# A hybrid convolution, attention and expert block on one core: channel tile 0 of the convolution moved to two other engines, and four edits to the start and the passes of the expert stage

## The reference

```python
u = rms_norm(x, norm1_g)
proj = u @ w_in                        # 1024 conv columns, 512 q, 128 k, 128 v
val, gate = proj[..., :512], proj[..., 512:1024]
z = val * sigmoid(gate)                # GLU
z = causal_depthwise_conv(z, conv_w) + conv_b      # 31 taps, 512 channels
conv_out = silu(layer_norm(z))
attn_out = swa_sink_attention(q, k, v) # 8 heads, chunks of 64, window of two chunks
h = x + concat(conv_out, attn_out) @ w_out
v = rms_norm(h, norm2_g)
gates, experts = softmax(top4(v @ router_w + router_b))        # 32 experts
y = h + sum over the 4 experts of gate * (clamped_swiglu(v @ w1[e] + b1[e]) @ w2[e] + b2[e])
```

## Time and profile before

| | |
|---|---|
| median of three runs | 2154.91 us |
| the profiled execution | 2154.91 us, its span from the first to the last instruction 2153.2 us |
| busy: PE, DVE, ACT, POOL | 2020.3, 932.0, 397.5, 228.1 us |
| chain that ended last | PE 82%, DVE 10%, issue 3%, ACT 2%, DMA 1%, POOL 1% |
| chain by line | PE L1001 46%, PE L1041 11%, PE L1016 10%, DVE L740 5% |
| start of the passes | 561.59 us after the span's start |

### The profile page before, as it was taken

One profiled execution on the slowest core, in us unless ns is written; L12 is line 12 of the kernel. 1 busy time (PEld: TensorE's weight loads), 2 busy tenths in 40 slices (PEclk: granted clock), 3 DMA queues, 4 the chain that ended last, 5 costly groups with the idle time before them and its releaser, 6 DMA issues.

```text
span 2153.2 us, 34646 instructions
## 1 busy us (share of the span) xinstructions
PE 2020.3 (94%) x13213; PEld 1648.4 (77%) x13214; DVE 932.0 (43%) x2247; ACT 397.5 (18%) x849; POOL 228.1 (11%) x223
## 2 busy tenths in 40 slices
PE   5997887899799999999999999999999999998997
PEld 3444543444677887788878887999999999988997
DVE  2895667333444444444443444333333333333221
ACT  3113334311111111111111111121111111110111
POOL 3101110000101010011101010011000000000000
PEclk9998889998799999999999999999999999999999
DMA  5020003212599899998999899988788887775651
GB/s 224 1 78 0 1 1 134 87 66 99 195 328 336 304 327 329 337 326 305 327 338 332 298 338 328 322 286 300 275 279 275 279 280 260 267 266 166 237 176 41
DMA packets 226274, 492.44 MB, mean 229 GB/s; under 512 B 7469, under 2 KB 8009, under 8 KB 226224
## 3 DMA queue, kind: packets, MB, share of 16 engines
q1 hardware_dynamic: 207504, 431.24, 55.5%
q0 software_dynamic: 16768, 59.98, 10.2%
q10 hardware_dynamic: 1952, 0.49, 0.1%
HBM read 458.88 MB, written 32.80 MB: 228 GB/s over the span
## 4 chain that ended last, share of the span: by engine, by line
PE 82%; DVE 10%; issue 3%; ACT 2%; DMA 1%; POOL 1%; ACTq 0%; DVEq 0%; POOLq 0%
PE bank L1001 46%; PE bank L1041 11%; PE bank L1016 10%; DVE arena L740 5%; PE bank L1215 5%; PE bank L1335 2%; PE bank L1136 1%; PE bank L1120 1%; ACT arena L543 1%; PE bank L1269 1%; PE bank L1029 1%; DVE arena L769 1%; DVE arena L785 1%; DVE mx L774 1%; PE bank L1307 1%
## 5 line engine op out<-in xcount | busy, mean ns | idle before, releaser
L1001 PE MATMUL bank<-arena 128*128 128x128 f32 (+5 forms) x8192 | 998.4, 284 | 21.5 <-issue 21.5
L1001 PEld LDWEIGHTS bank<-arena 128*128 128x128 f32 x8192 | 989.3, 192 | 34.1 <-issue 34.1
L663 DVE TENSOR_SCALAR arena<-bank,b1c 128x256 f32<-128x256 f32 x256 | 123.8, 483 | 611.1 <-PE bank L1001 602.0
L430 ACT ACTIVATE arena<-arena 128x256 f32<-128x256 f32 x256 | 106.6, 417 | 866.7 <-DVE arena L663 784.0
L1041 PE MATMUL bank<-arena 128*128 128x512 f32 x576 | 262.1, 593 | 0.0
L1016 PE MATMUL bank<-arena 128*128 128x144 f32 (+4 forms) x1792 | 252.0, 294 | 4.6 <-DVE arena L675 4.4
L1016 PEld LDWEIGHTS bank<-arena 128*128 128x128 f32 x1792 | 237.1, 190 | 7.8 <-DVE arena L675 7.7
L973 DVE TENSOR_SCALAR arena<-bank,cols 128x256 f32<-128x256 f32 x256 | 112.1, 480 | 283.4 <-PE bank L1335 283.4
L320 POOL DMA_INDIRECT out<-arena,idx_cur x64 | 99.0, 1547 | 826.9 <-ACT arena L444 422.5
L1041 PEld LDWEIGHTS bank<-arena 128*128 128x128 f32 x576 | 102.5, 190 | 94.7 <-issue 90.4
L740 DVE SCALAR_TENSOR_TENSOR arena<-arena,cols 128x1024 f32<-128x1024 f32 x120 | 159.3, 1328 | 3.7 <-ACT arena L518 0.2
(11 more groups left out here) (222 smaller groups left out, 1108.8 us busy)
## 6 DMA issues: line engine op xcount, KB each, us to landing
arena<-in_w SPq DMA_DIRECT2D x192, 2048.0 KB, 11.9
arena<-in_x SPq DMA_DIRECT2D x16, 512.0 KB, 5.2
token_rows<-arena SPq DMA_DIRECT2D x8, 528.0 KB, 5.9
arena<-in_w_in SPq DMA_DIRECT2D x2, 2048.0 KB, 11.2
out<-arena SPq DMA_DIRECT2D x8, 512.0 KB, 2.9
arena<-in_w_in SPq DMA_DIRECT2D x1, 3072.0 KB, 23.3
arena<-in_w_out SPq DMA_DIRECT2D x1, 2048.0 KB, 9.5
arena<-in_w_out SPq DMA_DIRECT2D x2, 1024.0 KB, 15.6
```

The source lines that it names most:

```text
L430: a.activation(sg[:, m % 2, :], g1[:, m % 2, :], ACT.Sigmoid, scale=ALPHA).then_inc(sg_ready, 1)
L663: v.tensor_scalar(g1[:, r, :], bank[r][:, 0:SLOTS], b1c[:, m:m + 1], LIMIT, ALU.add, ALU.min).then_inc(g1_ready, 1)
L1001: last = mm(bank[m % 2][:, side * SLOTS:side * SLOTS + n], w1_sb[:, k, lo:lo + P], xT[:, k, 0:n], start=k == 0, stop=k == KD - 1)
```

## The change

1. Channel tile 0 of the convolution leaves DVE. ACT writes tap 0 as before and then, for each other tap, a copy of zT scaled by the weight into one of two new buffers, `tapped`; POOL adds it to cT[:, 0] (1024 tokens). The 30 adds stand in groups of five behind units 2 to 7 of `glu`, on both engines. DVE keeps tiles 1 to 3, now with their tap 0 too, a tensor_scalar. 49 of its 93 taps stand before the attention. Behind `norm_qk(0)` DVE waits for the last add.
2. SP no longer waits for the first gather before it loads the w2 of the first pass.
3. `add_b2` of the last tile stands ahead of the index list's end on DVE instead of behind it.
4. The xT of the first pass is taken out by DVE behind the table instead of by ACT beside it. PE does transposes 1 to 3 behind the table's second matmul.
5. `down_rows` of half b waits for `yt_ev` at q2 + b instead of q2.

```diff
+        tapped = [part(9.5, SEQ), part(23.5, SEQ)]
+        FIRST_TAPS = [(1 + 5 * max(i - 2, 0), 1 + 5 * max(i - 1, 0)) for i in range(2 * CT)]
@@ SP
             sp.wait_ge(wo_mm, 2 * NT)
-            sp.wait_ge(gath_in, 32)
             for c in range(2):
                 load_w2(sp, c, 0)
@@ POOL
             for i in range(2 * CT):
                 glu(i)
+                for j in range(*FIRST_TAPS[i]):
+                    pool.wait_ge(tap_ready, j + 1)
+                    if j >= 2:
+                        pool.wait_ge(tap_added, j - 1)
+                    pool.tensor_tensor(cT[:, 0, :], cT[:, 0, :], tapped[j % 2], ALU.add).then_inc(tap_added, 1)
@@ ACT, in unit i
-                if i % 2 == 1:
-                    c = i // 2
-                    a.wait_ge(z_ready, i + 1)
-                    a.activation(cT[:, c, :], zT[:, c, 0:SEQ], ACT.Identity, scale=col(CW + c * WIDTH), bias=col(CB + c)
-                                 ).then_inc(first_tap, 1)
+                for j in range(*FIRST_TAPS[i]):
+                    z = zT[:, 0, j:j + SEQ]
+                    if j == 1:
+                        a.wait_ge(z_ready, 2)
+                        a.activation(cT[:, 0, :], zT[:, 0, 0:SEQ], ACT.Identity, scale=col(CW), bias=col(CB)
+                                     ).then_inc(tap_ready, 1)
+                    if j >= 3:
+                        a.wait_ge(tap_added, j - 2)
+                    a.activation(tapped[j % 2], z, ACT.Copy, scale=col(CW + j)).then_inc(tap_ready, 1)
@@ ACT, ahead of the passes
-            for i in range(2):
-                a.wait_ge(h_out[i], 16 * (NT // 4))
-            for i in range(4):
-                a.wait_ge(xt_mm, i + 1)
-                (two activations into xT, then_inc(xt_ev, 1))
@@ DVE
-            taps = [(c, j) for c in range(CT) for j in range(1, WIDTH)]
+            taps = [(c, j) for c in range(1, CT) for j in range(WIDTH)]
             def tap(c, j):
-                if j == 1:
-                    v.wait_ge(first_tap, c + 1)
+                if j == 0:
+                    v.wait_ge(z_ready, 2 * (c + 1))
+                    link(v.tensor_scalar(cT[:, c, :], zT[:, c, 0:SEQ], col(CW + c * WIDTH), col(CB + c), ...))
...
-            some_taps(2 * (WIDTH - 1) + 9)
+            some_taps(WIDTH + 18)
             norm_qk(0)
+            v.wait_ge(tap_added, WIDTH - 1)
...
             one_hots()
+            add_b2(NT - 1)
...
             second().then_inc(idx_ready, 1)
-            add_b2(NT - 1)
...
+            for i in range(4):
+                take_xT(0, i)
@@ PE
             def down_rows(b, ms):
                 if 0 in ms:
                     pe.wait_ge(w2_in[b], q16)
-                    pe.wait_ge(yt_ev, q2)
+                    pe.wait_ge(yt_ev, q2 + b)
...
             pe.wait_ge(gath_in, 32)
-            for i in range(4):
-                trans_x(0, i)
+            trans_x(0, 0)
             pe.wait_ge(diag_ready, 2)
             mm(bank[1][:, 0:5 * TQ + 4], ones_f[:], diag[:], start=True, stop=True).then_inc(tab_mm, 1)
+            for i in range(1, 4):
+                trans_x(0, i)
```

More of the change, by code:

```diff
@@ L194, in hybrid_block @@
         wcv_in, wqkv_in, wo_in = sem("wcv_in"), sem("wqkv_in"), sem("wo_in")
-        first_tap = sem("first_tap")
+        tap_ready, tap_added = sem("tap_ready"), sem("tap_added")
         rows_in, small_in = sem("rows_in"), sem("small_in")
@@ L228, in hybrid_block @@
         dve_own, act_own, pool_own, dve_loop = sem("dve_own"), sem("act_own"), sem("pool_own"), sem("dve_loop")
+        FIRST_TAPS = [(1 + 5 * max(i - 2, 0), 1 + 5 * max(i - 1, 0)) for i in range(2 * CT)]
+        assert FIRST_TAPS[-1][1] == WIDTH
         N_ROWS, N_SMALL = 10, 4
@@ L731, in _ @@
             last.then_inc(b1_done, 1)
-            taps = [(c, j) for c in range(CT) for j in range(1, WIDTH)]
+            taps = [(c, j) for c in range(1, CT) for j in range(WIDTH)]
             def tap(c, j):
-                if j == 1:
-                    v.wait_ge(first_tap, c + 1)
-                link(v.scalar_tensor_tensor(cT[:, c, :], zT[:, c, j:j + SEQ], col(CW + c * WIDTH + j), cT[:, c, :],
-                                            ALU.mult, ALU.add))
+                if j == 0:
+                    v.wait_ge(z_ready, 2 * (c + 1))
+                    link(v.tensor_scalar(cT[:, c, :], zT[:, c, 0:SEQ], col(CW + c * WIDTH), col(CB + c),
+                                         ALU.mult, ALU.add))
+                else:
+                    link(v.scalar_tensor_tensor(cT[:, c, :], zT[:, c, j:j + SEQ], col(CW + c * WIDTH + j),
+                                                cT[:, c, :], ALU.mult, ALU.add))
             def some_taps(n):
```

## The result

The changed kernel took 2223.46 us (median of 4, 2219.02 to 2230.05), the kernel before in the same comparison 2157.54 us. The ratio is 1.0312, with a 95% interval from 1.0291 to 1.0335: 67.3 us slower, between 63 and 72.

The account below looks back on a forecast made before the run. PE was taken to bound the passes, and DVE's taps the stage before norm_qk(0). Terms 46.6 - 6.9 + 3.3 + 24.3 = 67.3 us on 2154.9 gave 2222 us; the 8-in-10 range was 2196 to 2240.

Parts of the forecast that it names:

- The turn of tap and add: Convolution taps: DVE's tap and POOL's add alternate, 3.28 us a turn, DVE losing 1.96 per add; norm_qk(0) 46.6 us later.
- rival (d): Convolution taps: a POOL instruction holds DVE off for its whole length, 2.33 us an add; 11 us more, 2233 us; chance 0.13.
- The end of the taps: Behind norm_qk(0): 44 taps remain instead of 51, so the last tile's softmax waits less, -6.9 us.
- The wait in each narrow pass: Edit 5: PE waits for ACT to take bank 4, 1.35 us in each of 18 passes, +24.3 us.
- cover: Hand-over: 3.6 us between gather landing and the table's matmul input, behind 1.1 of transposes, hide edit 2's delay; cost 0.

Follow-up runs that it names:

- half adds: Kernel before with edit 1 only, each of the 30 POOL adds over 512 of 1024 tokens: 2.22 us a turn, constants to norm_qk(0) 119.48 us.
- the first profile of before: The unchanged kernel before, its first profiled execution: 2154.91 us. A second run of it, unchanged, measured 2156.21 us.
- edit 1 alone: Kernel before with only tile 0 of the convolution moved to ACT and POOL: 2200.36 us, ratio 1.0207 (1.0184 to 1.0229).

## Why the prediction was right

- **The number.** The mechanisms of edits 1, 4 and 5 were right, each with its size, and edits 1 and 5 carry it: in the changed kernel 47.3 - 6.8 + 23.1 = 63.6 us, and with 2.3 from the hand-over 65.9. The exact 67.3 is luck: the interval is 63 to 72, and the profiled pair differs by 70.2, with +4.1, -1.9, +3.6 and -1.0 in stages for which the forecast had no term.
- **The turn of tap and add.** Forecast 3.28 us from glu's rows of 512 tokens, measured 3.29. The choice that carried it was to take POOL's own increase with the tokens instead of DVE's 0.89 doubled (3.10). The half adds show the same increase from the other side. norm_qk(0) came 47.3 us behind its time instead of 46.6. By rival (d) it would have been 57. That is the whole-length lock that the Trainium skill states (SBUF — State Buffer, "SBUF: two separate sides"): the engines exclude each other as the page says, but an add that takes 2.35 us alone holds a tap off for 1.97, and a one-input instruction of 2.77 for 0.66.
- **The end of the taps.** Forecast -6.9 us, measured -6.8 between norm_qk(7) and the maximum.
- **The wait in each narrow pass.** Forecast 1.35 us a pass, measured 1.33. The 1.22 us until ACT has ended is exact. The weight load that no longer runs ahead was put at 0.2 to 0.4 us and cost 0.11; the 1.35 was right because it was set below the prediction's own two parts, which add up to 1.42 at least.
- **Edit 4.** Forecast +3.3 us, measured 3.3 alone, in part by two errors that cancel: from the end of the last transposes to the first pass it took 2.2 us, where 2.9 were forecast (562.1 to 565.0), and the first profile of before, from which it was worked out, had the stage 0.5 us longer than other executions (27.02, 26.47). In the changed kernel the stage as a whole lost 2.3 us against 26.5, for the next two reasons.
- **Edit 3.** Forecast 0. The prediction counted the 1.3 us of `add_b2` ahead of the index list and forgot that they leave the chain behind it. That chain is what the start of the passes waits for once edit 4 is in, and there the edit gains 1.3 us.
- **Edit 2.** Forecast 0 under cover, and in the changed kernel it costs 0.5 us. The cover was argued wrongly: I named 3.6 us behind the gather in the old order, where the transposes already filled them, and edits 2 and 3 cost 3.0 us there. Only edit 4's order, in which a single group of transposes stands in front of the table's matmul, gives most of the cover, and edit 3 takes 1.3 us of it away.
- **What the forecast had no term for.** The layer norm and projection stage was 3.6 us longer, of which the kernel before shows 2.3 by itself in another execution. The remaining 1.3 stay open; edit 1 alone has them too (194.05 us against 192.74). The first pass began at 609.64 us, not at the 604.6 forecast; 4.1 of that is the longer start.

## What to carry to other kernels

Before work is moved from VectorE to GpSimd to balance them, look for one row where both run together: the instruction that was stretched gives the price of the move, and here an add on GpSimd cost VectorE 1.97 us to save a tap of 1.316. A wait that seems harmless, on an engine that never stopped otherwise, cost its full length in each pass here, and the length could be read from where the other engine's instruction ends. And whether a transfer is covered depends on the order of what hangs on it: count the work between its landing and the point where the other chain arrives, not the gap between the two.

## What the runs showed of the hardware

- A VectorE tap and a GpSimd instruction take turns, and GpSimd keeps VectorE off for less than its own length. An add of 1024 tokens (2.35 us alone) costs a two-input VectorE instruction 1.97 us, a multiply or add of 512 tokens (1.26) 0.89, so 0.37 or 0.38 less than its length in both. A one-input instruction of 1024 tokens (2.77) costs 0.66, and an add of one token (0.19) nothing that could be told. GpSimd waits as well: that add of one token takes 1.29 us a turn beside taps of 1.28.
- A VectorE instruction with one input is held off too: tap 0, a tensor_scalar of 1024 tokens, took 2.81 us beside an add and 0.81 alone.
- A GpSimd tensor_scalar of 1024 float32 a partition took 2.77 us alone, longer than the tensor_tensor add of the same size (2.35).
- The gather of 256 rows took 8.29 us from its last issue to the first use with w2's load requested beside it, in the changed kernel 8.81, and 5.3 to 6.2 in the nine executions of complete kernels without.
- ACT's issue of one small transfer took between 0.60 and 6.7 us in different executions with no change to it or to what stands before it. The first unit of glu began at 47.2 to 48.2 us where it took at most 1.31, and at 51.1 to 52.8 where it took 5.5 or more.
